# Adding the squares of a layer's first norm on VectorE before one product with ones

## What is computed

```python
def rms_norm(x, g):
    y = xf * lax.rsqrt(jnp.mean(xf * xf, axis=-1, keepdims=True) + NORM_EPS)
    return (y * g).astype(x.dtype)

for i in range(DEPTH):                       # mixers a, b, c, a
    h = rms_norm(x, norm_pre[i])
    y = mixer(h, w_in, ..., w_out)
    x = x + rms_norm(y, norm_post[i])
```

## Time and profile before

| | |
|---|---|
| time before, median of 3 runs | 2730.25 us (2728.62 to 2730.37) |
| span of the profiled execution | 2726.5 us |
| TensorE matmul busy | 2497.7 us, 92% |
| VectorE busy | 1328.3 us, 49% |
| ScalarE busy | 755.7 us, 28% |
| GpSimd busy | 967.8 us, 35% |
| TensorE's share of the chain that ended last | 74%, of it 63% in L423 |
| mean granted TensorE clock | 0.957 of 2.4 GHz |

### The profile page before, as it was taken

The page is one execution under the profiler, slowest core; times in us unless marked ns, Lnnn a source line. Parts: engine busy times, 40 slices in busy tenths (PEclk is TensorE's granted clock), DMA queues, the critical chain, the costliest instruction groups (busy, mean ns, idle before and its releaser), DMA issues.

```text
span 2726.5 us, 38148 instructions
## 1 busy us (share of the span) xinstructions
PE 2497.7 (92%) x15108; PEld 2376.9 (87%) x15108; DVE 1328.3 (49%) x1528; ACT 755.7 (28%) x1033; POOL 967.8 (35%) x436
## 2 busy tenths in 40 slices
PE   8999999998997999777898979797999999998995
PEld 7998999998995999555786979795998999998994
DVE  3443443445246451888427867526443434445145
ACT  4222212122213113555223045424222121222111
POOL 3333333332334433222234335334333333332334
PEclk9999999999998999888898989898999999999997
DMA  5111111111122331000212101212111111111122
GB/s 185 45 46 36 40 45 39 38 39 39 44 81 110 108 85 55 22 0 0 78 46 80 46 31 39 96 47 90 44 46 46 39 39 38 39 39 39 46 79 86
DMA packets 46909, 149.41 MB, mean 55 GB/s; under 512 B 9040, under 2 KB 10984, under 8 KB 46696
## 3 DMA queue, kind: packets, MB, share of 16 engines
q1 hardware_dynamic: 27360, 99.66, 11.4%
q10 hardware_dynamic: 19472, 48.65, 5.1%
HBM read 121.98 MB, written 22.59 MB: 53 GB/s over the span
## 4 chain that ended last, share of the span: by engine, by line
PE 74%; DVE 9%; issue 8%; DVEq 3%; POOL 2%; ACT 2%; ACTq 1%; DMA 1%; POOLq 0%
PE ps L423 63%; PE ps L521 3%; PE ps L476 2%; POOL l_sc L377 2%; PE ps L704 2%; DVE x L1154 2%; PE ps L470 1%; PE ps L512 1%; DVE l_h_lo L1130 1%; DVE l_y_lo L1269 1%; DVEq L1155 1%; DVEq L1543 1%; DVEq L1547 1%; DVE l_hs L1558 1%; PE ps L455 0%
## 5 line engine op out<-in xcount | busy, mean ns | idle before, releaser
L351 POOL TENSOR_TENSOR w_hi<-w_raw,zero 128x1024 fp32r<-128x1024 f32 x182 | 348.0, 1912 | 1493.6 <-PE ps L423 1400.0
L423 PE MATMUL ps<-l_h_hi,w_hi 128*128 128x344 f32 x3024 | 649.7, 323 | 3.2 <-DVEq L1161 1.8
L423 PE MATMUL ps<-l_h_lo,w_hi 128*128 128x344 f32 x3024 | 643.1, 321 | 0.0
L423 PE MATMUL ps<-l_h_hi,w_lo 128*128 128x344 f32 x3024 | 638.1, 319 | 0.0
L423 PEld LDWEIGHTS ps<-l_h_hi,w_hi 128*128 128x128 f32 x3024 | 506.7, 188 | 9.4 <-issue 4.0
L423 PEld LDWEIGHTS ps<-l_h_lo,w_hi 128*128 128x128 f32 x3024 | 512.6, 189 | 0.0
L423 PEld LDWEIGHTS ps<-l_h_hi,w_lo 128*128 128x128 f32 x3024 | 504.2, 188 | 0.0
L354 POOL TENSOR_TENSOR w_lo<-w_raw,w_hi 128x1024 fp32r<-128x1024 f32 x182 | 445.4, 2447 | 14.3
L1160 DVE TENSOR_TENSOR l_tmp<-ps,rx 128x1032 f32<-128x1032 f32 x96 | 118.3, 1233 | 445.1 <-PE ps L423 444.9
L423 PE MATMUL ps<-l_y_hi,w_hi 128*128 128x344 f32 x1152 | 254.5, 326 | 37.4 <-ACT l_y_hi L861 17.0
L423 PE MATMUL ps<-l_y_hi,w_lo 128*128 128x344 f32 x1152 | 250.9, 323 | 0.0
(11 more groups left out here) (216 smaller groups left out, 2982.8 us busy)
## 6 DMA issues: line engine op xcount, KB each, us to landing
w_raw<-in_wu SPq DMA_DIRECT2D x182, 512.0 KB, 3.5
x_save<-x ACTq DMA_DIRECT2D x32, 516.0 KB, 2.6
x<-x_save ACTq DMA_DIRECT2D x32, 516.0 KB, 6.0
x<-in_xt SPq DMA_DIRECT2D x8, 516.0 KB, 8.5
l_sw<-l_q ACTq DMA_DIRECT2D x32, 129.0 KB, 2.3
out_y<-x ACTq DMA_DIRECT2D x8, 516.0 KB, 2.6
l_kc<-in_kcd ACTq DMA_DIRECT2D x1, 1024.0 KB
l_cos<-in_cos ACTq DMA_DIRECT2D x1, 516.0 KB, 3.5
```

Of the source, the lines that this page charges most:

```text
L351: nc.gpsimd.tensor_tensor(w_hi[:, j].rearrange("p k m -> p (k m)"), w_raw[:, j].rearrange("p k m -> p (k m)"), zeros, ALU.add).then_inc(w_ ...
L423: mm = nc.tensor.matmul(ps[:, 3 * slot + ch, 0:CW], wt[:, w, k, :], mv[:, k, ch * CW:(ch + 1) * CW], start=(k == 0 and t == 0), stop=(k == ...
```

## The change

The squares of a layer are now added over the 8 tiles on VectorE into a new tile `tot`; TensorE multiplies ones with `tot` once per layer. The buffer of squares is given back to ScalarE (`sq_used`) by VectorE and no longer by TensorE. A new semaphore `tot_done` says that `tot` is complete.

```diff
@@ first_unit, TensorE
                     if k == KT - 1:
                         mm.then_inc(result, 1)
-                    pe.wait_ge(*L.sq_done.at(k + 1))
-                    for bank, col, tok, n in STAT:
-                        mm = nc.tensor.matmul(ps[:, bank, col:col + n], ones[:, :], sq2[:, k % 2, tok:tok + n],
-                                              start=(k == 0), stop=(k == KT - 1))
-                        if k == KT - 1 and bank != 6:
-                            mm.then_inc(L.ssq_mm.sem, 1)
-                    if k < KT - 2:
-                        mm.then_inc(L.sq_used.sem, 1)
+                pe.wait_ge(*L.tot_done.at(1))
+                column_sums(tot, L.ssq_mm)
                 pe.wait_ge(*L.root.at(1))
@@ pre, VectorE
                     V.scalar_tensor_tensor(L.h_lo[:, k, :], x[:, k, :], g_pre[:, L.i, k:k + 1], L.h_hi[:, k, :],
                                            ALU.mult, ALU.subtract).then_inc(L.h_done.sem, 1)
+                    dve.wait_ge(*L.sq_done.at(k + 1))
+                    if k:
+                        V.drain()
+                    add_up(tot, sq2[:, k % 2, :], k == 0)
+                    if k < KT - 2:
+                        V.drain().then_inc(L.sq_used.sem, 1)
+                V.drain().then_inc(L.tot_done.sem, 1)
                 dve.wait_ge(*L.rx_done.at(1))
```

More of the change, by code:

```diff
@@ L69 @@
     "hi_done": (KT, KT, KT), "h_done": (KT, KT, KT), "sq_done": (KT, KT, KT), "sq_used": (KT - 2, KT - 2, KT - 2),
-    "ssq_mm": (2, 2, 2), "root": (2, 2, 2), "rx_done": (1, 1, 1),
+    "ssq_mm": (2, 2, 2), "tot_done": (1, 1, 1), "root": (2, 2, 2), "rx_done": (1, 1, 1),
     "x_saved": (16 * KT,) * 3, "x_back": (16 * KT,) * 3, "in_done": (3 * MA, 2 * KT + 2, KT), "act_done": (MA, KT, 0),
@@ L139, in build @@
         corner = keep("corner", [P, 4])
+        tot = keep("tot", [P, NT])
         ps = ctx.enter_context(nc.psum_tensor("ps", [P, 8, 512], F32))
@@ L175, in build @@
             L.sq_used, L.ssq_mm, L.root, L.rx_done = s("sq_used"), s("ssq_mm"), s("root"), s("rx_done")
-            L.rp_done, L.scaled = s("rp_done"), s("scaled")
+            L.rp_done, L.scaled, L.tot_done = s("rp_done"), s("scaled"), s("tot_done")
             L.x_saved, L.x_back = s("x_saved"), s("x_back")
```

## The result

| | before | changed |
|---|---|---|
| median of 4 runs, us | 2729.43 (2727.79 to 2730.37) | 2740.69 (2737.24 to 2742.44) |
| span of the profiled execution, us | 2726.5 | 2737.6 |
| mean granted TensorE clock | 0.957 | 0.952 |

The changed kernel is slower: ratio 1.0041, 95% interval 1.0027 to 1.0055, so +11.3 us where +18.1 was forecast. The spans differ by 11.1. (Around the span of a single execution lie 1.8 us: 2739.43 - 2737.6. The 3.75 us that the part ahead of the prediction gave for this also held 2 us of scatter between executions; the forecast is the median before plus 18.1, so it doesn't hang on that.)

The account below looks back on a forecast made before the run. VectorE was to become what the heads of layers 1 to 3 wait for: +5.1, +5.1, +3.4, with layer 0's -1.8, make +11.8 us at full clock; +6.3 for the clock gives +18.1, so 2748 us, range 2740 to 2757.

Parts of the forecast that it names:

- What bounds the head: Heads of layers 1 to 3: VectorE at 4.12 us per tile becomes the bound, above TensorE's 3.36.
- The turns with GpSimd: Layer 1's head: VectorE gets seven turns beside GpSimd's scaling before and after; the copy shortens its turn by 0.6 us.
- The sum at full clock: All four heads with TensorE at 2.4 GHz: +5.1, +5.1, +3.4 and -1.8 us, together +11.8.
- The +3.4 of layer 3: Layer 3's head: +5.1 us less 1.7 us already lost at half clock in the kernel before.
- Layer 0: Head without x updates: VectorE's 2.71 us per tile is under TensorE's 3.36, so the product with ones ends 1.8 us earlier.
- 3 x 1.94 + 0.5 = 6.3 us: Heads of layers 1 to 3 end at half clock: 1.94 us more per product with ones, 0.5 us more in layer 1's second unit.
- bounds of 0 and 1.9 us: Layer 0's head: extra time for a lower TensorE clock, 0 at full clock and 1.9 us at half.
- The clock stays at full: Rival, chance 0.20: TensorE keeps full clock in the heads of layers 1 to 3; +11.8 us, 2742.
- More meetings with GpSimd: Rival, chance 0.08: additions in the heads meet GpSimd more often, 25 x 1.3 = 32 us more, 2780.
- Faster: Rival, chance 0.07: TensorE stays the heads' bound, gaining up to 54.3 us (2676); needs an addition at 0.75 us or less.
- No change: Rival, chance 0.07: additions don't take turns with GpSimd, saving 14.4 us; +3.7 us, 2734.

Follow-up runs that it names:

- The kernel with the products kept: Changed kernel with all eight products with ones per layer kept on TensorE beside the additions; 2749.26 us, ratio 1.0076.
- the one without additions: Changed kernel without its seven additions per layer, tot only a copy of the last tile's squares (wrong sums); 2705.08 us, ratio 0.9911.
- the one with two of each: Changed kernel with each of the seven additions per layer done twice (wrong sums); 2786.89 us, ratio 1.0214.

## Why the prediction was right, and where it was off

*What bounds the head.* Right for layers 1 to 3. It became VectorE, at 4.16 us per tile (forecast 4.12). The kernel with the products kept shows it from one side (TensorE's work doesn't matter), the one without additions and the one with two of each from the other (VectorE's does).

*The turns with GpSimd.* Right: seven turns as before, the additions in them 3.23 us, those behind them 1.23. The copy shortened GpSimd's phase by 0.56 us (forecast 0.6).

*The sum at full clock.* Forecast +5.1, +5.1 and +3.4 in layers 1 to 3; measured +5.5, +5.5 and +3.8. Some 0.2 of the 0.4 in layer 1 is the pitch, five tiles at 0.04; `tot` came 47.3 us after VectorE's first instruction, 47.1 forecast; the other 0.2 lie between `tot` and the second unit. The +3.4 of layer 3 deserves a remark: it relied on a clock loss in the kernel before that moves to another layer from one execution to the next. Over the three layers together it matters little: the heads before sum to 132.1 us in the first profile and 133.1 in the second.

*Layer 0.* Forecast -1.8 at full clock, measured -1.6, and that agreement is luck. The -1.6 holds a product with ones at half clock, 0.7 us that were gained behind the head, and VectorE being early. What VectorE did in layer 0's head of the changed kernel:

```profile
23.44 2.74 DVE L1145 TENSOR_TENSOR tot<-tot,sq 128x1032 f32<-128x1032 f32 x1
26.31 3.17 DVE L1125 SCALAR_TENSOR_TENSOR l_h_lo<-x,g_pre,l_h_hi 128x1032 fp32r<-128x1032 f32 x1
```

The split met addition 5 and h_lo 6, not h_lo 5 and addition 5, and cost 1.5 + 1.9 = 3.4 us and not 4.2, so `tot` was complete at 33.35 where 34.3 was forecast. In the second profile, with the product at full clock, the head is 34.85, 2.4 us under its counterpart (37.20) and 2.7 under the first (37.54).

*The clock: the step that was mis-sized.* The term "3 x 1.94 + 0.5 = 6.3 us" rested on "I take it that these heads end at 0.50". TensorE's clock did fall, and most of the head ran at 0.50, but the term was worth nothing in layers 1 to 3. While VectorE is the bound, TensorE's clock costs time only in what comes behind `tot`: the one product with ones and the first matmuls after it, and there the clock was back.

What I overlooked in VectorE's order: behind addition 6 no update of x is left, so h_lo 7 starts 889.33 - 886.79 = 2.54 us after h_lo 6 and not 4.16; TensorE, at half clock, worked without a gap from 888.14 to 891.94 and had 2.4 GHz at 892.04. That this gapless stretch is what brought the clock back is argued from the order of the rows and not shown. For it speaks the kernel with two additions, which puts a wait of 1.4 to 3.5 us in that place and has half clock behind it in all four heads. Against it as a rule speak two places of the changed kernel. In layer 0 the same gapless work, 29.54 to 33.34 us, was followed by half clock in the first profile and by 2.4 GHz in the second. And in layer 1's head the clock had come back once before, at 875.66, behind a wait of 1.21 us. So that the clock was back at the end of six heads of six is measured, and why is open.

For layer 0 the prediction had bounds of 0 and 1.9 us; the two profiles of the changed kernel show a product at 2.4 and one at 1.2 GHz, 1.6 us apart. The Trainium skill (TensorE: Matmul & The Clock Gate, "Why this matters for your kernels") says to avoid idle gaps between bursts of matmuls, since the clock falls back. As the prediction applied it, every head's end would have been at the lower level; here it came out so in none of six, and in one of two for layer 0.

*Luck.* Of the 7 us between forecast and time (2748 and 2740.69) the clock term accounts for 6.3. The rest of the sum, +11.8, comes within 0.5 us of the +11.3 measured partly because two errors cancel: the three heads lost 1.3 us more than forecast, and layer 1's rest gave back 2.1 that no term had. The time is inside the range of 2740 to 2757 by 0.7 us only; the second group of runs of the same kernel, at 2737.24, would have been outside.

*The rivals.* "The clock stays at full" came out in its number (2742 against 2740.69), though not in its words: the clock did fall, only not where it counts. "More meetings with GpSimd" didn't come; in layers 1 to 3 the additions behind its phase are at 1.23 us. "Faster" needed an addition at 0.75 us or less; the free ones took 1.23. "No change" falls with the 3.23 us of the additions in the phase of turns.

*Not forecast.* Layer 1's rest is 2.1 us shorter (1.8 in the second pair of profiles). It holds the attention, where the granted clock differs. The stretch from 1090 to 1240 in the kernel before:

```profile
1090.00:1240.00 150.00, 116.83 (x438) 79.60 (x439) 125.87 (x423) 80.69 (x261) 40.24 (x22) 0.87 0.04 11
```

And in the changed kernel:

```profile
1090.00:1240.00 150.00, 102.86 (x431) 69.45 (x432) 124.05 (x410) 81.35 (x260) 42.50 (x23) 0.95 0.05 15
```

The clock there is 0.87 in both profiles of before and 0.95 and 0.93 in the changed kernel's. But the kernels without additions and with two tiles on VectorE had 0.99 in the same stretch, and their rests of layer 1 are longer than the one before, 541.9 and 542.0, so this doesn't explain the 2 us, and their cause stays open.

## What to carry to other kernels

Work taken off the busiest engine counts only down to the next engine's time per tile, here 0.75 us of reserve, and moving it onto just that engine spends the reserve and more (1.34 us per tile here). Before work is moved, write down both engines' time per tile in every phase of the stage, and move as many tiles as balance them: two or three of eight gained 0.4 to 0.5% where all eight lost 0.4%. A lower clock costs time only at an instruction that the end hangs on, so it has to be priced there and not over the stretch in which it is seen.

## What the hardware showed that was not expected

- The granted clock went 0.51, 1.00, 0.51, 1.00 within 34 us at the end of one head, and TensorE's busy share was lower in the stretch at 1.00 (4.39 of 10 us) than in the two at 0.51 (5.90 of 13 and 4.88 of 7). The end of it, at 2.4 GHz, repeated in six heads of six.
- Behind one and the same wait of 3.04 us, in two executions of one kernel, the clock was once at 2.4 and once at 1.2 GHz; the loss is 2.7 us in that head (43.5 and 46.2). Behind one and the same gapless work of 3.8 us in layer 0 it was once at 1.2 and once at 2.4.
- VectorE and GpSimd, each with a stream of instructions without gaps, took turns so evenly that a VectorE instruction took 3.2 us beside GpSimd whether it was an addition (3.23), an update of x (3.18) or an h_lo (3.20), and only the copy took less (2.88).
